# Feed-forward hidden tiles in parts of 4, 6, 6 and 6 in place of 4, 5, 6 and 7

## The chip, the cores and the metric

The kernel runs on one core of a Trainium2 chip. The metric is the device time of one execution, in microseconds (us). Three runs of the kernel before gave a median of 2325.38 us, from 2324.81 to 2325.91.

The engines are named as the profile names them: PE (TensorE, matmuls), PEld (its weight loads), ACT (ScalarE), DVE (VectorE), POOL (GpSimd) and SP (SyncE, which here issues nearly all transfers). Each engine works through its own list of instructions in order. They wait for each other through counting semaphores.

## What is computed

Four layers; each is a token mixer (attention, gated unit, pooling, attention) and a feed-forward part, all on 512 tokens of width 1024 in float32. Only the feed-forward part, whose hidden width is 2816, or 22 tiles of 128, is touched by the change:

```python
FFN_HIDDEN = -(-8 * D_MODEL // (3 * 256)) * 256          # 2816

def swiglu(h, w_gate_up, w_down):
    g, u = jnp.split(h @ w_gate_up, 2, axis=-1)
    return (jax.nn.silu(g) * u) @ w_down

# in reference(), once for each layer i
x = x + m
x = x + swiglu(rmsnorm(x, ffn_norm[i]), ffn_w_gate_up[i], ffn_w_down[i])
```

## The kernel before

**Precision.** Each float32 operand of a matmul is split into a high part, rounded by an ACT copy, and a low part, which DVE gets as the difference. A product is three matmuls: high by high, high by low, low by high. So every weight that a transfer brings passes ACT and then DVE before PE may use it.

**Parts.** The 22 hidden tiles of a layer are done in four parts, p = 0 to 3. A part first computes its hidden tiles (gate and linear columns, silu, product) and then multiplies them by its rows of `w_down`: eight blocks, one for each tile of the output, each added to `x` by DVE (`add`, line 1208). A block of a part of n tiles is 3n matmuls of 512 columns.

**Part 0** (4 tiles) computes gate and linear in the plain way, from the operand in `xs_hi`/`xs_lo`. Meanwhile ACT and DVE build from `x` the sums of token halves that the later parts need.

**Parts 1 to 3** compute each hidden tile as a *pair* (its gate and its linear columns) with seven products in place of eight (Winograd's form of Strassen's scheme). They are called s1, s2, a11, s4, s3, a12, a22, in this order. Each is 12 matmuls of 256 columns, so a pair is 84 matmuls. The weights of a pair are 512 rows of sums (`s32`, built by DVE in `pair_sums`, lines 1233 to 1239) and of raw columns. They are split in four *chunks* c = 0 to 3: the high part by ACT (`pair_high`, line 737), the low part by DVE (`pair_low`, line 1245). s1 and s3 read chunk 0, s2 and s4 chunk 1, a11 and a12 chunk 2, a22 chunk 3. ACT also copies four finished products out of PSUM (`snap`, line 814). PE waits for the first copy before s4, for the second before s3, for the third before a12 and for the fourth before a22.

**Two homes for a pair's split weights.** One is the ring of four slots `w_hi`/`w_lo`, which also holds the split weights of the `w_down` blocks. The other is the space of `xs_hi`/`xs_lo`, free after part 0's gate and linear blocks. The pairs of a part take turns, and the last must be in `xs`, since the ring is then needed for `w_down`:

```python
def pair_slot(p, j):                  # 1: xs_hi/xs_lo, 0: the ring
    return (PAIRS[p] - j) % 2
```

Chunk c of a part's first pair (j = 0) may be written at these points (in `pair_high`, lines 730 to 736; `plain_before(l, p)` counts the blocks up to the part's start, `block_done` those that PE has done):

```python
elif pair_slot(p, j) == 0:
    act.wait_ge(block_done, plain_before(l, p) - 3 + c)
elif c == 0:
    if p == 1:
        act.wait_ge(block_done, plain_before(l, 0))
    else:
        act.wait_ge(product_done, 7 * pair_at(l, p))
```

So in the ring, chunk c waits for the fifth, sixth, seventh and eighth `w_down` block of the part before, since each of these blocks reads one slot.

**The order around part 0's end** is written out by hand, in `first_tiles` of ACT and of DVE. `up` is the layer's first feed-forward block; the `w_down` blocks of part 0 are `up + 8` to `up + 15`. ACT, from line 794:

```python
split(up + 14, ...); pair_high(l, 1, 0, 0); pair_high(l, 1, 0, 1)
split(up + 15, ...); pair_high(l, 1, 0, 2); pair_high(l, 1, 0, 3)
```

DVE, from the sums of the first pair on:

```python
pair_sums(l, 1, 0); add(2); split(up + 14, ...); pair_low(l, 1, 0, 0)
add(3); split(up + 15, ...); token_part_low(2, 1); add(4)
pair_low(l, 1, 0, 1); pair_low(l, 1, 0, 2); add(5); pair_low(l, 1, 0, 3)
b21_low(); add(6); pair_sums(l, 1, 1); add(7)
```

After that ACT enters the loop over the part's pairs. For pair j it first splits chunk 0 of pair j + 1, then takes the first copy `snap(q, 2)`, splits chunks 1 and 2, takes the second copy `snap(q, 1)`, splits chunk 3, and takes the third and fourth copy. Chunk 0 and chunk 1 of pair j + 1 wait for `pair_sums` of that pair on DVE.

**Transfers.** SP loads raw pairs alternately into `raw_b` (even j) and `raw_a` (odd j). `raw_a` is the space of the two buffers `raw` for plain blocks, so the load of pair 1 of a part waits until DVE has split the last `w_down` block (`w_lo_ready`).

Of the kernel before, what the change touches and what calls it, by code (L numbers as in the profile page):

```python
# [37 lines left out]
HEADS, GROUPS, DH = 16, 4, 64  # L38
NCMP = 32
HIDDEN_TILES = 22  # L40
PARTS = (4, 5, 6, 7)
TILES_AT = (0, 4, 9, 15)
LAST_PART = len(PARTS) - 1
FIRST_TILES = PARTS[0]
PAIRS = (0, 5, 6, 7)
PAIRS_AT = (0, 0, 5, 11)
LAYER_PAIRS = sum(PAIRS)
H = 256
BW = 1024
# [9 lines left out]
MIX_BLOCKS = {"nsa": 38, "sgu": 25, "pool": 18}  # L59
FFN_BLOCKS = 2 * FIRST_TILES + MT * len(PARTS)  # L60

# [38 lines left out]
class Plan:  # L100
# [35 lines left out]
    def width(self, b):  # L136
# [3 lines left out]
        for at in self.ffn:  # L140
            p, k = divmod(b - at - 2 * FIRST_TILES, MT)
            if 0 <= p <= LAST_PART:
                return PARTS[p] * P
        return BW
# [13 lines left out]
def pair_at(l, p, j=0):  # L158

    return LAYER_PAIRS * l + PAIRS_AT[p] + j  # L160


def pair_slot(p, j):

    return (PAIRS[p] - j) % 2


def loads_before(q):

    l, r = divmod(q, LAYER_PAIRS)  # L170
    buf = [j % 2 for n in PAIRS for j in range(n)]
    return l * buf.count(buf[r]) + buf[:r].count(buf[r])
# [79 lines left out]
def build(nc, x_in, positions, stream, pairs, params, consts, b_s, out, mixers=MIXERS):  # L252
    plan = Plan(mixers)
    ctx = ExitStack()
    with ctx:  # L255
# [260 lines left out]
        def _(sp):  # L516
# [20 lines left out]
            def loads(lo, hi):  # L537
                for b in range(lo, hi):
                    if b in plan.plain:
                        load_plain(b)  # L540
                    else:
                        load(b, (b - plan.skipped(b)) % RAW)
# [15 lines left out]
            for l in range(len(mixers)):  # L558
# [3 lines left out]
                loads(up + 4, up + 2 * FIRST_TILES + MT)  # L562
                for p in range(1, len(PARTS)):
                    n = PAIRS[p]
                    for j in range(1, n):
# [99 lines left out]
        def _(act):  # L665
# [78 lines left out]
            def down_high(l, p, k):  # L744

                if k < RING:
                    act.wait_ge(product_done, 7 * (pair_at(l, p, PAIRS[p] - 2) + 1))
                b = plan.down_block(l, p) + k
# [52 lines left out]
            def ffn(l):  # L801
                n = norm_of_ffn(l)
                first_tiles(l)
                for p in range(1, len(PARTS)):
                    tiles = count = PARTS[p]
                    t0 = HIDDEN_TILES * l + TILES_AT[p] + tiles - count
                    down = plan.down_block(l, p)
# [311 lines left out]
        def _(dve):  # L1119
# [260 lines left out]
            def ffn(l):  # L1380
# [3 lines left out]
                for p in range(1, len(PARTS)):  # L1384
                    tiles = count = PARTS[p]
                    t0 = HIDDEN_TILES * l + TILES_AT[p] + tiles - count
                    down = plan.down_block(l, p)
# [511 lines left out]
        def _(pe):  # L1899
# [152 lines left out]
            def ffn(l):  # L2052
# [10 lines left out]
                for p in range(1, len(PARTS)):  # L2063
                    for j in range(PAIRS[p]):
                        pair(l, p, j)
                    down, t0 = plan.down_block(l, p), HIDDEN_TILES * l + TILES_AT[p]
                    for k in range(MT):
# [371 lines left out]
def _tiles(w, nk=MT):  # L2439

    K, M = w.shape
    b = w.reshape(K // P, P, M // P, P).transpose(2, 1, 0, 3).reshape(M // P, P, (K // P) * P)
    return _pad(b)
# [11 lines left out]
def _stream(i, mixers, total):  # L2455
    out = []
    for l, (kind, j) in enumerate(mixers):
# [26 lines left out]
        out.append(both.reshape(2 * FIRST_TILES, P, BW))  # L2484
        for n, t in zip(PARTS, TILES_AT):
            out.append(_tiles(down[t * P:(t + n) * P]))
# [85 lines left out]
```

## Time and profile before

| | |
|---|---|
| median of three runs | 2325.38 us |
| the profiled execution | 2326.84 us |
| its span, first to last instruction | 2325.0 us |
| PE busy | 2313.3 us, 99% |
| PEld busy | 2078.9 us, 89% |
| DVE busy | 1737.7 us, 75% |
| ACT busy | 1131.9 us, 49% |
| mean granted clock of TensorE | 0.999 |

The matmuls are pipelined and overlap in the records, so a short wait of PE need not show as idle time. It shows as a larger step from the start of one matmul to the start of the next: in steady work 0.227 us for 512 columns and 0.120 us for 256.

### The profile page before, as it was taken

The page shows a single profiled execution, that of the slowest core. Times are in us where ns is not written, and L with a number is a line of the kernel's source. Part 1 is how long each engine was busy: PE and PEld are TensorE (multiplying, and loading weights), DVE is VectorE, ACT ScalarE, POOL GpSimd, SP SyncE. Part 2 cuts the span into 40 slices and gives each one's busy share as a digit, 9 for nine tenths or more (in the row PEclk, how much of TensorE's full clock was granted, in tenths as well). Part 3 has the DMA queues.
Part 4 walks back from the last instruction along what each step waited for, and adds up shares of the span by engine and source line. Part 5 has one row for each costly group of instructions (what it writes and reads, how often), then busy time and mean ns, then how long its engine had stood idle before and what let it go on. Part 6 is the DMA issues. An engine that isn't in the chain of part 4 may idle for free.

```text
span 2325.0 us, 37973 instructions
## 1 busy us (share of the span) xinstructions
PE 2313.3 (99%) x14360; PEld 2078.9 (89%) x14360; DVE 1737.7 (75%) x2847; ACT 1131.9 (49%) x1944; POOL 308.1 (13%) x305
## 2 busy tenths in 40 slices
PE   9999999999999999999999999999999999999998
PEld 7889988999988889999988899998889998899997
DVE  8667668876965679687777897696756776978693
ACT  6268744544543335454533454454326783454453
POOL 2211140000030120000123000003320114000003
PEclk9999999999999999999999999999999999999999
DMA  4820013333323233333233333332470003223332
GB/s 160 220 64 2 1 56 100 114 96 102 114 84 102 89 108 100 99 109 110 78 97 100 99 111 100 95 116 84 123 209 28 1 2 98 89 93 102 98 101 84
DMA packets 69295, 217.38 MB, mean 93 GB/s; under 512 B 8193, under 2 KB 8321, under 8 KB 69121
## 3 DMA queue, kind: packets, MB, share of 16 engines
q1 hardware_dynamic: 62928, 204.39, 27.7%
q0 software_dynamic: 5184, 8.40, 1.8%
q8 instruction: 116, 1.90, 0.3%
q10 hardware_dynamic: 1008, 2.21, 0.3%
q14 instruction: 59, 0.48, 0.1%
HBM read 204.48 MB, written 2.10 MB: 89 GB/s over the span
## 4 chain that ended last, share of the span: by engine, by line
PE 77%; DVE 0%; ACT 0%; issue 0%; DVEq 0%; ACTq 0%
PE bank L1901 76%; PE bank L2241 2%; PE bank L2271 0%; DVE branch L1666 0%; DVE big L1894 0%; ACT L695 0%; DVE w_lo L1245 0%; ACT w_hi L737 0%; ACT xg L1108 0%; DVE act_t L1398 0%; DVE x L1208 0%; DVEq L255 0%; DVE rden L1661 0%; DVE rden L1663 0%; PE bank L2145 0%
## 5 line engine op out<-in xcount | busy, mean ns | idle before, releaser
L679 ACT ACTIVATE w_hi<-raw 128x1024 fp32r<-128x1024 f32 (+4 forms) x260 | 239.6, 922 | 297.0 <-DMA raw<-stream 238.3
L1141 DVE TENSOR_TENSOR w_lo<-raw,w_hi 128x1024 fp32r<-128x1024 f32 (+4 forms) x257 | 287.9, 1126 | 112.8 <-ACT w_hi L679 112.4
L1901 PE MATMUL bank<-hid_hi,w_hi 128*128 128x512 f32 x720 | 280.9, 390 | 0.0
L1901 PE MATMUL bank<-hid_lo,w_hi 128*128 128x512 f32 x720 | 280.5, 390 | 0.0
L1901 PE MATMUL bank<-hid_hi,w_lo 128*128 128x512 f32 x720 | 280.3, 389 | 0.0
L1901 PE MATMUL bank<-xs_hi,w_hi 128*128 128x512 f32 (+2 forms) x720 | 279.2, 388 | 0.8 <-DVE w_lo L1141 0.5
L1901 PE MATMUL bank<-xs_lo,w_hi 128*128 128x512 f32 (+2 forms) x720 | 273.4, 380 | 0.0
L1901 PE MATMUL bank<-xs_hi,w_lo 128*128 128x512 f32 (+1 forms) x704 | 267.5, 380 | 0.0
L1208 DVE TENSOR_TENSOR x<-bank,x 128x512 f32<-128x512 f32 (+1 forms) x160 | 110.2, 689 | 198.7 <-PE bank L1901 198.3
L1901 PE MATMUL bank<-mix_hi,w_hi 128*128 128x256 f32 (+1 forms) x768 | 246.0, 320 | 0.0
L1901 PE MATMUL bank<-mix_hi,w_lo 128*128 128x256 f32 (+1 forms) x768 | 244.8, 319 | 0.0
L1901 PE MATMUL bank<-mix_lo,w_hi 128*128 128x256 f32 (+1 forms) x768 | 244.8, 319 | 0.0
L595 POOL TENSOR_TENSOR work<-x 128x512 f32<-128x512 f32 x8 | 15.0, 1877 | 1390.6 <-DVE x L1208 1306.7
L814 ACT ACTIVATE part_sums<-bank 128x256 f32<-128x256 f32 x288 | 108.5, 377 | 165.7 <-PE bank L1901 165.4
L1642 DVE CUSTOM_DVE_ANT_0 attn<-bank,causal_b 128x512 f32<-128x512 f32 (+3 forms) x256 | 118.8, 488 | 84.7 <-PE bank L1901 83.9
L1901 PE MATMUL bank<-mix_hi,xs_hi 128*128 128x256 f32 x640 | 181.3, 283 | 0.2 <-DVE w_lo L1245 0.2
L1901 PE MATMUL bank<-mix_hi,xs_lo 128*128 128x256 f32 x640 | 181.3, 283 | 0.0
L1901 PE MATMUL bank<-mix_lo,xs_hi 128*128 128x256 f32 x640 | 181.3, 283 | 0.0
L1901 PE MATMUL bank<-tmp,attn 128*128 128x65 f32 x1280 | 162.8, 268 | 0.0
L1901 PEld LDWEIGHTS bank<-xs_hi,w_hi 128*128 128x128 f32 (+1 forms) x720 | 135.1, 188 | 29.4 <-DVE xs_lo L1149 1.5
L1901 PEld LDWEIGHTS bank<-hid_hi,w_hi 128*128 128x128 f32 x720 | 135.2, 188 | 29.2 <-DVE hid_lo L1405 1.5
L1901 PEld LDWEIGHTS bank<-hid_hi,w_lo 128*128 128x128 f32 x720 | 135.2, 188 | 28.0
(280 smaller groups left out, 5878.8 us busy)
## 6 DMA issues: line engine op xcount, KB each, us to landing
raw<-stream SPq DMA_DIRECT2D x131, 512.0 KB, 3.7
raw_b<-pairs SPq DMA_DIRECT2D x80, 512.0 KB, 4.8
raw_a<-pairs SPq DMA_DIRECT2D x64, 512.0 KB, 4.6
raw<-stream SPq DMA_DIRECT2D x32, 448.0 KB, 3.4
raw<-stream SPq DMA_DIRECT2D x32, 384.0 KB, 3.1
raw<-stream SPq DMA_DIRECT2D x32, 320.0 KB, 2.9
w_f<-stream SPq DMA_DIRECT2D x18, 512.0 KB, 3.7
raw<-stream SPq DMA_DIRECT2D x34, 256.0 KB, 2.6
```

Of the source, the lines that this page charges most:

```text
L595: gp.tensor_tensor(work[:, 0, :], x[:, 0, :], x[:, 0, :], ALU.mult).then_inc(sq_step, 1)
L679: nc.scalar.activation(w_hi[:, slot, 0:n], raw[:, k, 0:n], ACT.Copy).then_inc(w_hi_ready, 1)
L814: nc.scalar.activation(part_sums[:, i, :], src[:, 0:H], ACT.Copy).then_inc(snapped, 1)
L1141: nc.vector.tensor_tensor(w_lo[:, slot, 0:n], raw[:, k, 0:n], f32(w_hi[:, slot, 0:n]), ALU.subtract).then_inc(w_lo_ready, counted(b))
L1208: nc.vector.tensor_tensor(tile(x, m), bank[slot][:, :], tile(x, m), ALU.add).then_inc(taken, 1)
L1642: nc.vector.tensor_tensor_reduce(out=prob[:, p % 4, bass.ts(j, w)], in0=bank[score_bank(l0, p)][:, bass.ts(j, w)], in1=causal_b[:, S - w:S ...
L1901: return nc.tensor.matmul(out_, w, v, start=start, stop=stop, skip_group_check=onto)
L2241: last = nc.tensor.transpose(bank[turn_bank(l0, p)][:, bass.ts(k, P)], prob[:, p % 4, bass.ts(k, P)], ident[:, :])
```

## The change

```diff
-PARTS = (4, 5, 6, 7)
-TILES_AT = (0, 4, 9, 15)
+PARTS = (4, 6, 6, 6)
+TILES_AT = (0, 4, 10, 16)
 LAST_PART = len(PARTS) - 1
 FIRST_TILES = PARTS[0]
-PAIRS = (0, 5, 6, 7)
-PAIRS_AT = (0, 0, 5, 11)
+PAIRS = (0, 6, 6, 6)
+PAIRS_AT = (0, 0, 6, 12)
```

The number of pairs of a layer (18), of blocks and of matmuls stays. A tile moves from the last part to the first of the three; the widths of `w_down`'s blocks follow (640, 768 and 896 columns become 768 each). Since 5 and 7 are odd and 6 is even, `pair_slot(p, 0)` goes from 1 to 0 in parts 1 and 3: their first pair moves from `xs` to the ring, and with it every later pair of part 1 and of part 3 changes home.

ACT, at the end of part 0 in layer 0, before (line 679 splits a plain block, 737 a chunk of a pair, 814 is the copy of a product out of PSUM; `block_done` counts PE's blocks):

```order
L679 ACTIVATE w_hi<-raw 128x512 [waits block_done,raw_full1]
L737 ACTIVATE xs_hi<-s32_58 128x1024 [waits block_done,s_ready]
L737 ACTIVATE xs_hi<-s32_58 128x1024 [waits s_ready]
L679 ACTIVATE w_hi<-raw 128x512 [waits block_done,raw_full0]
L737 ACTIVATE xs_hi<-raw_b 128x1024 [waits pair_full_b]
L737 ACTIVATE xs_hi<-raw_b 128x512
L737 ACTIVATE w_hi<-s32_58 128x1024 [waits block_done,s_ready]
L814 ACTIVATE part_sums_63<-bank45 128x256 [waits product_done,hid_full]
```

The same place on ACT now:

```order
L679 ACTIVATE w_hi<-raw 128x512 [waits block_done,raw_full1]
L737 ACTIVATE w_hi<-s32_58 128x1024 [waits block_done,s_ready] x2
L679 ACTIVATE w_hi<-raw 128x512 [waits block_done,raw_full0]
L737 ACTIVATE w_hi<-raw_b 128x1024 [waits block_done,pair_full_b]
L737 ACTIVATE w_hi<-raw_b 128x512 [waits block_done]
L737 ACTIVATE xs_hi<-s32_58 128x1024 [waits block_done,s_ready]
L814 ACTIVATE part_sums_63<-bank45 128x256 [waits product_done,hid_full]
```

No instruction changes its place; the four chunks of the first pair go to `w_hi`, and each of them now waits for a block of PE, where before only the first did, and for a much earlier one.

DVE, a little behind it in the program, as the difference of the two (line 1293 is `token_part_low`, 1208 `add`, 1245 `pair_low`, 1312 `b21_low`):

```order
 L1293 TENSOR_TENSOR b_lo_60<-b32_59,b22_hi_61 128x1024
 L1208 TENSOR_TENSOR x<-bank2,x 128x512
-L1245 TENSOR_TENSOR xs_lo<-s32_58,xs_hi 128x1024
-L1245 TENSOR_TENSOR xs_lo<-raw_b,xs_hi 128x1024
-L1208 TENSOR_TENSOR x<-bank3,x 128x512
-L1245 TENSOR_TENSOR xs_lo<-raw_b,xs_hi 128x512
+L1245 TENSOR_TENSOR w_lo<-s32_58,w_hi 128x1024
+L1245 TENSOR_TENSOR w_lo<-raw_b,w_hi 128x1024
+L1208 TENSOR_TENSOR x<-bank3,x 128x512
+L1245 TENSOR_TENSOR w_lo<-raw_b,w_hi 128x512
 L1312 TENSOR_TENSOR b_lo_60<-b32_59,xs_hi 128x512
 L1312 TENSOR_TENSOR b_lo_60<-b32_59,xs_lo 128x512
```

Here too the order stands as it was; the low parts go to `w_lo`, and each follows ACT's high part of the same chunk.

## Rows read from the trace of the kernel before

**Rows 1.** The page, part 1: busy us, share of the span, instructions
```profile
PE 2313.3 (99%) x14360; PEld 2078.9 (89%) x14360; DVE 1737.7 (75%) x2847; ACT 1131.9 (49%) x1944; POOL 308.1 (13%) x305
```

**Rows 2.** Waits of PE, longest first: total us, times, longest
```profile
PE bank L2145 <- ACT tmp L890: 1.6, 1, 1.6
```

**Rows 3.** Windows of layer 0: busy of PE, PEld, DVE, ACT, POOL; clock; DMA
```profile
395.14:416.90 21.76, 21.76 (x97) 18.03 (x96) 21.49 (x29) 8.09 (x12) 0.00 (x0) 1.00 0.36 111
416.90:467.30 50.40, 50.40 (x422) 50.39 (x421) 42.54 (x59) 28.32 (x53) 0.00 (x0) 1.00 0.32 105
467.30:494.78 27.48, 27.48 (x123) 22.45 (x121) 16.98 (x22) 7.41 (x9) 0.00 (x0) 1.00 0.27 86
```

**Rows 4.** Timeline of PE, layer 0: start us, us, instruction
```profile
395.14 0.39 PE L1901 MATMUL bank<-hid_hi,w_hi 128*128 128x512 f32 x1
...
416.90 0.28 PE L1901 MATMUL bank<-mix_hi,xs_hi 128*128 128x256 f32 x1
...
421.22 0.28 PE L1901 MATMUL bank<-b_hi,xs_hi 128*128 128x256 f32 x1
```

**Rows 5.** Timeline of DVE, layer 0, part 0's end and part 1's first pair
```profile
406.95 1.22 DVE L1245 TENSOR_TENSOR xs_lo<-s,xs_hi 128x1024 fp32r<-128x1024 f32 x1
...
408.68 0.68 DVE L1141 TENSOR_TENSOR w_lo<-raw,w_hi 128x512 fp32r<-128x512 f32 x1
...
416.29 1.22 DVE L1233 TENSOR_TENSOR s<-raw_a 128x1024 f32<-128x1024 f32 x1
...
427.92 0.69 DVE L1398 TENSOR_TENSOR act_t<-act_t,lin 128x512 f32<-128x512 f32 x1
```

**Rows 6.** Timeline of ACT, the same stretch; in brackets idle before, and releaser
```profile
407.01 0.62 ACT L679 ACTIVATE w_hi<-raw 128x512 fp32r<-128x512 f32 x1
...
417.54 1.06 ACT L737 ACTIVATE w_hi<-s 128x1024 fp32r<-128x1024 f32 x1 [8.44 <-DVE s L1233]
418.60 0.38 ACT L814 ACTIVATE part_sums<-bank 128x256 f32<-128x256 f32 x1
418.99 1.06 ACT L737 ACTIVATE w_hi<-s 128x1024 fp32r<-128x1024 f32 x1
419.96 1.05 ACT L737 ACTIVATE w_hi<-raw_a 128x1024 fp32r<-128x1024 f32 x1
420.91 0.36 ACT L814 ACTIVATE part_sums<-bank 128x256 f32<-128x256 f32 x1
...
421.69 0.37 ACT L814 ACTIVATE part_sums<-bank 128x256 f32<-128x256 f32 x1
...
431.34 0.38 ACT L814 ACTIVATE part_sums<-bank 128x256 f32<-128x256 f32 x1
```

**Rows 7.** Timeline of ACT, layer 0, part 1's end: part 2's first pair
```profile
491.64 1.06 ACT L737 ACTIVATE w_hi<-raw_b 128x1024 fp32r<-128x1024 f32 x1 [1.68 <-PE bank L1901]
494.98 0.64 ACT L737 ACTIVATE w_hi<-raw_b 128x512 fp32r<-128x512 f32 x1 [2.28 <-PE bank L1901]
```

**Rows 8.** Timeline of PE, layer 0: part 1's first `w_down` block; part 2's second pair
```profile
469.82 0.39 PE L1901 MATMUL bank<-hid_hi,w_lo 128*128 128x512 f32 x1
...
470.50 0.39 PE L1901 MATMUL bank<-hid_lo,w_hi 128*128 128x512 f32 x1
...
510.49 0.28 PE L1901 MATMUL bank<-b_hi,xs_lo 128*128 128x256 f32 x1
...
511.14 0.28 PE L1901 MATMUL bank<-mix_lo,xs_hi 128*128 128x256 f32 x1
```

**Rows 9.** The transfers into `raw_a`, by tile; and DVE's timeline at part 2
```profile
DMA to landing us min/median/max: 3.8/4.6/6.5
503.62 1.23 DVE L1233 TENSOR_TENSOR s<-raw_b 128x1024 f32<-128x1024 f32 x1 [0.81 <-DMA raw_b<-pairs]
```

**Rows 10.** PE's longest wait, layer 0's mixer: timeline, and its window
```profile
114.87 0.44 PE L2145 MATMUL bank<-ident,tmp 128*128 128x128 f32 x2 [1.55 <-ACT tmp L890]
112.00:120.00 8.00, 6.45 (x34) 4.44 (x33) 5.04 (x7) 2.90 (x5) 0.00 (x0) 1.00 0.43 137
```

## The prediction

> **What bounds the kernel now.** I read the page first, then PE's waits, then the windows of one layer's parts, then the timelines of PE, DVE and ACT side by side at the borders between parts. PE is busy for 99% of the span [rows 1], and its longest wait in the whole trace is 1.6 us [rows 2]. Busy time alone would prove little, because the matmuls overlap in the records, so I look at steps from start to start. Five pairs of part 1 take 50.40 us [rows 3], which is 10.08 us a pair, 84 steps of 0.120, 1.44 us a product. The eight `w_down` blocks of part 0 run from 395.14 to 416.90 [rows 4], 2.72 us each, 12 steps of 0.227. There is nothing between them. PE sets the time here, and the change leaves its matmuls as they are. So it can cost or give only what PE waits at borders.
>
> The second thing to see is how near DVE is to its limit at the border that the change touches. In the window of part 0's `w_down` blocks DVE is busy for 21.49 of 21.76 us [rows 3]. From 408.68 (the low split of the eighth block) to 416.29 (`pair_sums` of part 1's second pair) it works without a gap [rows 5]. ACT has 8.09 us to do in the same window, and PE still never waits. In the pairs behind it DVE has 42.54 of 50.40 us [rows 3].
>
> **What goes.** Two small waits of PE end with the part of 5 tiles. In its first `w_down` block the fifth tile's input is late: two steps take 470.50 − 469.82 = 0.68 us in place of 2 × 0.227 [rows 8], so 0.23 us are lost. It stands at the same two matmuls of this part in each of the four layers. With 6 tiles the input is asked for three matmuls, 0.68 us, later. That gives 4 × 0.23 = 0.92 us. In layer 0, part 2's second pair also loses 511.14 − 510.49 − 2 × 0.12 = 0.41 us [rows 8]. It hangs on a late transfer (in part 2, DVE waits 0.81 us for `raw_b` [rows 9]), whose issue waits on the first pair's last chunk on DVE. Behind blocks of 6 tiles, DVE has 0.68 us more per block before that point, so I count these 0.41 us as gone too. Together 1.33 us. The last part's blocks become shorter by 3 matmuls, the first part's longer by as many; PE's sum over them is the same, so they stand at nothing.
>
> **What comes: part 1's first pair must wait for the ring.** I work it out in layer 0; the other layers hold the same instructions. Part 0's fifth to eighth blocks end at 408.74, 411.46, 414.18 and 416.90 (416.90 less 3, 2, 1 and 0 blocks of 2.72). A chunk's high copy starts 0.20 to 0.29 us behind its block where a first pair already lies in the ring: in part 2, 494.98 behind the last block's end at 494.78, and 491.64 behind the seventh's at 494.78 − 27.48 / 8 = 491.35 [rows 3, 7]. I take 0.25.
>
> - DVE comes to the low part of chunk 0 at 406.95 as before [rows 5], but ACT's copy can start only at 408.99 and takes 1.06. So DVE stands still from 406.95 to 410.05.
> - ACT is in order: chunk 1 is queued ahead of the eighth block's split. Chunk 1 starts at 411.46 + 0.25 = 411.71. The split follows 0.97 later (418.99 to 419.96 is such a step) at 412.68, and takes 0.62 [rows 6]: 413.30. DVE, which has `add(3)` behind it by 411.8, stands still again until 413.33.
> - From this split to `pair_sums` of the second pair DVE has the same ten instructions as before, 416.29 − 408.68 = 7.61 us [rows 5]. Chunks 2 and 3 do not hold it up: their copies are done by 415.5 and 417.8, and DVE, with the lengths of rows 5 (1.22 for 1024 columns, 0.68 for 512, of which some 0.08 overlap), comes to them at about 416.8 and 418.5. `pair_sums` starts at 413.33 + 7.61 = 420.94, which is 4.65 us later than before.
> - ACT waits for it, and with ACT the copies out of PSUM. Chunk 0 of the second pair started 1.25 us behind `pair_sums` (417.54), the first copy 1.06 later (418.60, 0.38 long) [rows 6]. With 4.65 us more the first copy ends at 423.63. PE wants to begin the fourth product, s4, at 421.22 [rows 4]. It waits 2.43 us with 0.02 for the signal.
> - The second copy, at 420.91 + 4.65, ends at 425.92 [rows 6]. PE is through s4 at 423.65 + 1.44 = 425.09 and wants s3: another 0.85 us. The third copy (421.69) ends at 426.71, before s3 is done at 427.38, so a12 does not wait. The first pair ends at 416.90 + 10.08 + 3.28 = 430.26.
> - In the second pair PE is 3.28 late and DVE 4.65, since from `pair_sums` to the product of silu and linear (416.29 to 427.92 [rows 5]) it had no gap to make good. The second copy of this pair, 431.34 to 431.72 before [rows 6], ends at 436.37. PE wants s3 at 430.26 + 4 × 1.44 = 436.02: 0.37 us. From there on DVE's spare time (7.86 us in five pairs) takes up the rest.
>
> In sum 2.43 + 0.85 + 0.37 = 3.65 us a layer, 14.6 in four layers. The eighth block's low split is now done at 414.02 where PE wants it at 414.18. That leaves 0.16 us of cover, so I put it at nothing, with up to 0.1 us a layer beyond. What cover is there elsewhere: chunks 0 to 2 are ready at least 1.4 us before their products ask for them, and chunk 3 earlier still.
>
> **Parts 2 and 3.** Part 2's first pair was in the ring already. Part 3's moves there. But at this border the order by hand has chunks 0 and 1 behind the sixth block's `add`, chunk 2 behind the seventh's, chunk 3 behind the eighth's. So the ring's wait is one that DVE mostly passes in any case, and in part 2 PE loses nothing for it in the first pair. I take zero, with 0 to 0.4 us a layer (the loss in rows 8) as bounds.
>
> **The sum.** 14.6 − 1.33 = 13.3 us. The profiled execution took 2326.84, 1.84 beyond its span of 2325.0; the median of the runs is 1.46 lower. The terms are differences within one execution, so I add them to the median: 2325.4 + 13.3 = 2338.7 us, 0.57% more.
>
> **Rivals.**
>
> *The wait is hidden, as at part 2.* Place: ACT's first copy in part 1's first pair. It costs PE nothing if that copy ends by 421.22, so if `pair_sums` starts by 421.22 − 0.38 − 1.06 − 1.25 = 418.53. My 420.94 would have to be 2.4 us too late. For it: in part 2 the same slots are waited for, and PE goes on. Against it: in part 2 `pair_sums` stands ahead of chunk 3, and here it stands behind all four chunks, two splits of other data and an `add`. Price: only the gains are left, 2325.4 − 1.3 = 2324.1 us, not slower. Chance 0.06.
>
> *The transfer of the second pair becomes the bound.* Its place `raw_a` is free when the eighth block is split, which moves from before 409.4 to 414.02. Such a load takes 3.8 to 6.5 us, 4.6 in the median [rows 9], so it lands between 417.8 and 420.5, and DVE asks for it at 420.94. For it: DVE did wait for a pair's transfer at part 2 [rows 9]. Against it: even the longest of 64 is in time. If it took 1 us more than the time that it has, 7.9 us, the loss would be 1 us a layer: 2342.7. Chance 0.10.
>
> *PE loses its fast clock in the wait.* Behind its longest wait before, 1.55 us, the granted clock of the window stayed at 1.00 [rows 10], its upper level of 2.4 GHz, and a wait of 2.43 us is not in the trace. The Trainium skill ("TensorE: Matmul & The Clock Gate", Part 1) holds that throttled is the default state of the array and that only activity keeps it fast. By that rule the time would be higher; the one row here that bears on it shows no loss. If the 2.4 GHz fell to 1.2 for one pair, that would be 10.08 us a layer: 2338.7 + 40 = 2379 us. Chance 0.03.
>
> *Less of it:* the second and third wait fail to come because ACT gets by sooner than I count; then 4 × 2.43 − 1.33 = 8.4, 2333.8 us. Chance 0.10, inside or just below the range.
>
> **How the numbers follow.** My forecast has 0.71; with the three other slower cases (0.10, 0.03, 0.10) slower has 0.94. No difference beyond 0.2%, 4.7 us, is about what a measurement here can tell from none. The hidden wait, 0.06, falls within it, but for 0.01 that I leave for faster: nothing in the rows gives 4.7 us back. The range goes from 2334.0 (the first wait alone) to 2343.0 (the late transfer); it leaves out the hidden wait and the clock.
>
> **What would show it.** On DVE two gaps before the low parts of chunk 0 and of the eighth block, about 3.1 and 1.5 us, and no gap then until `pair_sums` on `raw_a`, some 4.0 us behind part 1's start in place of 0.6 before it. On PE a step of about 2.5 us before the fourth product of part 1's first pair, one of about 1 before the fifth, and a small one before the fifth of the second pair, in all four layers. PE's waits name ACT's copies (line 814) with eight or more entries. The fifth tile's two steps are gone. I am wrong if the first pair of part 1 stays at 10.1 us, if part 2 or 3 shows waits of that size, or if the clock in these windows is under 1.

## The result, and the profile after

The changed kernel takes 2340.14 us in the median (2339.66 to 2340.93), against 2325.28 for the kernel before in the same session: a ratio of 1.0064, 95% interval 1.0047 to 1.0081. It is 14.9 us slower; 13.3 were forecast, and 2340.14 lies in the range. The profiled execution took 2339.66 us, its span is 2337.8.

The page looks almost as before. Its first part, in the same columns:

```profile
PE 2316.3 (99%) x14360; PEld 2081.0 (89%) x14360; DVE 1740.5 (74%) x2847; ACT 1134.6 (49%) x1944; POOL 305.0 (13%) x305
```

Set beside [rows 1], the engines have as many instructions as before, and PE is busy for 3.0 us more where the span grew by 12.8. What grew is the time between. Windows of layer 0, in the columns of [rows 3]: part 0's `w_down` blocks, the first and the second pair of part 1, its other four pairs, its `w_down` blocks:

```profile
393.28:415.08 21.80, 21.80 (x98) 17.94 (x96) 17.11 (x23) 7.91 (x11) 0.00 (x0) 1.00 0.23 68
415.08:428.56 13.48, 10.53 (x86) 10.18 (x85) 13.37 (x17) 6.11 (x11) 0.00 (x0) 1.00 0.43 139
428.56:439.04 10.48, 10.31 (x87) 10.13 (x86) 10.13 (x14) 6.00 (x11) 0.00 (x0) 1.00 0.38 125
439.04:479.36 40.32, 40.32 (x339) 40.32 (x338) 33.44 (x48) 23.06 (x43) 0.00 (x0) 1.00 0.32 108
479.36:512.02 32.66, 32.66 (x146) 27.04 (x145) 18.38 (x23) 7.95 (x9) 0.00 (x0) 1.00 0.27 81
```

The first pair takes 13.48 us in place of 10.08, the second 10.48, the other four 10.08 each. DVE's busy time in part 0's blocks fell from 21.49 [rows 3] to 17.11: work that it no longer gets done there lies in the first pair, where it is now busy for 13.37 of 13.48 us. The timeline of DVE shows where it stood still. In brackets: idle before, and what ended it.

```profile
404.55 0.68 DVE L1141 TENSOR_TENSOR w_lo<-raw,w_hi 128x512 fp32r<-128x512 f32 x1
408.24 1.23 DVE L1245 TENSOR_TENSOR w_lo<-s,w_hi 128x1024 fp32r<-128x1024 f32 x1 [3.00 <-ACT w_hi L737]
409.38 0.68 DVE L1208 TENSOR_TENSOR x<-bank,x 128x512 f32<-128x512 f32 x1
411.48 0.69 DVE L1141 TENSOR_TENSOR w_lo<-raw,w_hi 128x512 fp32r<-128x512 f32 x1 [1.41 <-ACT w_hi L679]
...
419.10 1.21 DVE L1233 TENSOR_TENSOR s<-raw_a 128x1024 f32<-128x1024 f32 x1
```

The two gaps are there, 3.00 and 1.41 us. `pair_sums` on `raw_a` starts 4.02 us behind part 1's start at 415.08; before, it started 0.61 us ahead of it [rows 4, 5]. There is no idle time in front of it, so the transfer into `raw_a` was in place. ACT, over the same border:

```profile
407.14 1.06 ACT L737 ACTIVATE w_hi<-s 128x1024 fp32r<-128x1024 f32 x1 [3.61 <-PE bank L1901]
409.86 1.06 ACT L737 ACTIVATE w_hi<-s 128x1024 fp32r<-128x1024 f32 x1 [1.66 <-PE bank L1901]
...
420.34 1.06 ACT L737 ACTIVATE xs_hi<-s 128x1024 fp32r<-128x1024 f32 x1 [4.43 <-DVE s L1233]
421.30 0.37 ACT L814 ACTIVATE part_sums<-bank 128x256 f32<-128x256 f32 x1
...
423.70 0.36 ACT L814 ACTIVATE part_sums<-bank 128x256 f32<-128x256 f32 x1
```

Chunks 0 and 1 wait for PE's blocks. Before, with part 1's start at 416.90, ACT had both done by 407.1, in one go and with no wait in front:

```profile
405.12 1.99 ACT L737 ACTIVATE xs_hi<-s 128x1024 fp32r<-128x1024 f32 x2
```

In the changed kernel ACT then waits 4.43 us for `pair_sums` of the second pair, and the two copies out of PSUM (line 814) stand behind it. PE goes on 0.10 and 0.11 us after they end:

```profile
419.27 0.28 PE L1901 MATMUL bank<-b_hi,w_lo 128*128 128x256 f32 x1
421.77 0.36 PE L1901 MATMUL bank<-b_hi,w_hi 128*128 128x256 f32 x1 [2.22 <-issue]
421.96 0.28 PE L1901 MATMUL bank<-b_lo,w_hi 128*128 128x256 f32 x1
...
423.16 0.28 PE L1901 MATMUL bank<-b_hi,w_lo 128*128 128x256 f32 x1
424.17 0.36 PE L1901 MATMUL bank<-mix_hi,w_hi 128*128 128x256 f32 x1 [0.73 <-DVE xs_lo L1245]
```

A step of 2.50 us in place of 0.12, and one of 1.01; each has a step of 0.19 behind it. PE's waits as the view lists them (total us, times, longest):

```profile
PE bank L1901 <- issue: 9.2, 5, 2.2
PE bank L1901 <- DVE xs_lo L1245: 1.5, 2, 0.7
```

The view does not name ACT's copies. It has "issue" for the long waits and a DVE instruction for the second one, because several semaphores are waited for there. The ACT and PE timelines side by side point to the copies, and e4 below bears it out: with the copies taken early, these two waits are gone.

Two layers hold something more. The windows of part 1's first pair in layer 2 and in layer 3:

```profile
1353.46:1367.42 13.96, 11.74 (x85) 11.56 (x84) 13.82 (x18) 6.11 (x11) 0.00 (x0) 0.88 0.45 141
2041.78:2056.16 14.38, 11.82 (x85) 11.38 (x84) 14.21 (x19) 6.11 (x11) 0.00 (x0) 0.88 0.48 151
```

The granted clock (the column before the DMA share) is 0.88 there, and 0.50 for a stretch of it, in layer 2 this one:

```profile
1360.00:1363.40 3.40, 3.25 (x15) 3.28 (x16) 3.40 (x5) 3.12 (x6) 0.00 (x0) 0.50 0.04 16
```

Four matmuls of layer 2's first pair in PE's timeline:

```profile
1360.15 0.55 PE L1901 MATMUL bank<-b_hi,w_hi 128*128 128x256 f32 x1 [2.22 <-issue]
1360.50 0.41 PE L1901 MATMUL bank<-b_lo,w_hi 128*128 128x256 f32 x1
1360.71 0.41 PE L1901 MATMUL bank<-b_hi,w_lo 128*128 128x256 f32 x1
...
1363.47 0.28 PE L1901 MATMUL bank<-mix_hi,w_hi 128*128 128x256 f32 x1
```

Behind the wait the steps are 0.213 us in place of 0.120, as long as the clock stands at 0.50, or 1.2 GHz in place of 2.4; from 1363.47 on they are 0.120 again.

### The profile page after: what moved, and what is told of

Read it like the earlier page. It is cut to its first block, busy times and chain, and to the rows that moved or that the text cites. A ratio compares the mean times of both kernels' runs of the same rounds, so it can differ in the third digit from the quotient of the medians.

```text
span 2337.8 us, 37973 instructions
## 1 busy us (share of the span) xinstructions
PE 2316.3 (99%) x14360; PEld 2081.0 (89%) x14360; DVE 1740.5 (74%) x2847; ACT 1134.6 (49%) x1944; POOL 305.0 (13%) x305
## 4 chain that ended last, share of the span: by engine, by line
PE 60%; DVE 0%; issue 0%; ACT 0%; DVEq 0%; ACTq 0%
PE bank L1901 58%; PE bank L2241 2%; PE bank L2271 0%; DVE branch L1666 0%; DVE big L1894 0%; ACT L695 0%; DVE w_lo L1245 0%; ACT w_hi L737 0%; ACT xg L1108 0%; DVE x L1208 0%; DVE act_t L1398 0%; DVE rden L1661 0%; DVEq L255 0%; DVE rden L1663 0%; PE bank L2145 0%
## 5 line engine op out<-in xcount | busy, mean ns | idle before, releaser
L679 ACT ACTIVATE w_hi<-raw 128x1024 fp32r<-128x1024 f32 (+2 forms) x260 | 239.8, 923 | 306.5 <-DMA raw<-stream 237.5
L1141 DVE TENSOR_TENSOR w_lo<-raw,w_hi 128x1024 fp32r<-128x1024 f32 (+2 forms) x257 | 290.1, 1134 | 118.1 <-ACT w_hi L679 117.5
L1901 PE MATMUL bank<-mix_hi,w_hi 128*128 128x256 f32 (+1 forms) x832 | 264.7, 318 | 1.8 <-DVE xs_lo L1245 1.5
L1901 PE MATMUL bank<-mix_lo,w_hi 128*128 128x256 f32 (+1 forms) x832 | 263.2, 316 | 0.0
L1901 PE MATMUL bank<-mix_hi,w_lo 128*128 128x256 f32 (+1 forms) x832 | 263.2, 316 | 0.0
L1901 PEld LDWEIGHTS bank<-mix_hi,w_hi 128*128 128x128 f32 x832 | 159.3, 191 | 12.9 <-DVE xs_lo L1245 2.4
L1901 PEld LDWEIGHTS bank<-mix_hi,w_lo 128*128 128x128 f32 x832 | 159.1, 191 | 10.2
L1901 PEld LDWEIGHTS bank<-mix_lo,w_hi 128*128 128x128 f32 x832 | 159.2, 191 | 10.0
L1901 PE MATMUL bank<-mix_hi,xs_lo 128*128 128x256 f32 x576 | 163.0, 283 | 0.0
L1901 PE MATMUL bank<-mix_lo,xs_hi 128*128 128x256 f32 x576 | 163.0, 283 | 0.0
```

Source lines behind the costliest of these rows:

```text
L679: nc.scalar.activation(w_hi[:, slot, 0:n], raw[:, k, 0:n], ACT.Copy).then_inc(w_hi_ready, 1)
L1141: nc.vector.tensor_tensor(w_lo[:, slot, 0:n], raw[:, k, 0:n], f32(w_hi[:, slot, 0:n]), ALU.subtract).then_inc(w_lo_ready, counted(b))
L1901: return nc.tensor.matmul(out_, w, v, start=start, stop=stop, skip_group_check=onto)
```

## The experiments

All times are medians, with the ratio to the kernel before on the same chip and its 95% interval.

**One border at a time.** The theory: all of the loss comes from part 1's first pair. The rival: a first pair in the ring costs at each border. Two other splittings of the tiles have one of the two borders each:

```diff
-PARTS = (4, 6, 6, 6)
+PARTS = (4, 6, 5, 7)      # e1: part 1's first pair in the ring, part 3's in xs
+PARTS = (4, 5, 7, 6)      # e2: part 3's first pair in the ring, part 1's in xs
```

> Parts of 4, 6, 5, 7: of the two borders that the change moves to the ring, only part 1's first pair is there; part 3's stays in xs. My theory (the loss is all at part 1's first two pairs): 3.8 us a layer as in the changed kernel, four times, 15.3; the late fifth tile is back, now in part 2 (no gain of 0.92), layer 0's 0.41 is gone: 2325.3 + 14.9 = 2340.2 us, up to 0.6 more if the clock falls again in two layers. Rival, that each of the two first pairs in the ring costs its share: 2325.3 + 7.4 = 2332.7 us.

Measured: 2343.96 us, 1.0082 (1.0068 to 1.0096). Layer 1, the first pair of part 1 and of part 3:

```profile
905.84:919.32 13.48, 10.52 (x85) 10.16 (x84) 13.38 (x17) 6.11 (x11) 0.00 (x0) 1.00 0.45 145
1080.67:1090.74 10.07, 10.07 (x85) 10.07 (x84) 9.68 (x13) 5.34 (x10) 0.00 (x0) 1.00 0.57 178
```

The whole loss is at part 1. The time is 3.2 us above the upper end of my expectation. In the profiled execution (2341.93 us) the clock fell in three layers, not two. The five runs follow the mean granted clock: 2341.65 us at 0.999, 2341.93 and 2343.96 at 0.997, 2345.24 at 0.995, 2346.60 at 0.994. What the slower of them look like inside was not recorded.

> Parts of 4, 5, 7, 6: only part 3's first pair is in the ring, part 1's and part 2's are in xs. My theory: no wait at part 3's border, 10.08 us a pair everywhere, the late fifth tile of part 1 as before: 2325 us, between 2324.4 and 2326. Rival, that a first pair in the ring costs wherever it stands: 2332.7 us.

Measured: 2324.69 us, 0.9997 (0.9988 to 1.0006). ACT's timeline before part 3 in layer 1:

```profile
1082.88 1.06 ACT L737 ACTIVATE w_hi<-raw_b 128x1024 fp32r<-128x1024 f32 x1 [3.70 <-PE bank L1901]
1087.58 0.63 ACT L737 ACTIVATE w_hi<-raw_b 128x512 fp32r<-128x512 f32 x1 [3.64 <-PE bank L1901]
```

and the windows of part 3's first two pairs:

```profile
1087.38:1097.45 10.07, 10.07 (x85) 10.06 (x84) 9.68 (x13) 5.90 (x11) 0.00 (x0) 1.00 0.61 189
1097.45:1107.53 10.08, 10.08 (x86) 10.08 (x85) 9.65 (x13) 6.00 (x11) 0.00 (x0) 1.00 0.33 104
```

ACT waits 3.70 and 3.64 us for the ring, and PE loses nothing here; over the four layers, only layer 2's second pair of part 3 is longer, by 0.11 us. So being in the ring is not by itself what costs. Two things differ at this border: DVE is busy for only 19.77 of the 38.11 us of part 2's blocks, and `pair_sums` stands ahead of chunk 3, so that it starts 2.26 us ahead of part 3's start at 1087.38:

```profile
1085.12 1.22 DVE L1233 TENSOR_TENSOR s<-raw_a 128x1024 f32<-128x1024 f32 x1
```

e6 below brings the second to part 1's border, without the first.

**The eighth block's split ahead of chunk 0.** If the transfer into `raw_a`, or the split of the eighth block, is what comes late, this takes the loss away; if it is DVE's order, only the second gap's share.

```diff
 # ACT                                    # DVE
+split(up + 15, ...)                      +add(3); split(up + 15, ...)
 pair_high(l, 1, 0, 0)                     pair_low(l, 1, 0, 0)
 pair_high(l, 1, 0, 1)                    -add(3); split(up + 15, ...)
-split(up + 15, ...)                       token_part_low(2, 1)
```

> The changed kernel, but the eighth w_down block of part 0 is split ahead of chunk 0 of the first pair, on ACT and on DVE. The load into raw_a goes out some 6 us sooner; DVE still stands before chunk 0, but not a second time. My theory (DVE comes late to pair_sums, PE pays for it through ACT's copies): pair_sums starts 0.85 us sooner, the first wait of PE falls from 2.45 to about 1.6 us, the other two (0.96 and 0.41) stay: 4 x 0.85 = 3.4 us less than the changed kernel, 2336.7 us. Rival, that the load into raw_a is what is late: all of the waits go, 2325 us. Rival, that the split of the eighth block on PE's side is what is late: 2325 us too.

Measured: 2336.28 us, 1.0046 (1.0033 to 1.0060). DVE and PE in layer 1:

```profile
897.73 1.23 DVE L1245 TENSOR_TENSOR w_lo<-s,w_hi 128x1024 fp32r<-128x1024 f32 x1 [1.85 <-ACT w_hi L737]
...
907.82 1.21 DVE L1233 TENSOR_TENSOR s<-raw_a 128x1024 f32<-128x1024 f32 x1
910.49 0.36 PE L1901 MATMUL bank<-b_hi,w_hi 128*128 128x256 f32 x1 [1.49 <-issue]
```

The load into `raw_a` now goes out 8.62 us ahead of part 1's start, in place of 2.89. `pair_sums` starts 907.82 − 904.53 = 3.29 us behind that start, 0.73 sooner than in the changed kernel (4.02), and PE's first wait shrinks by as much (2.22 to 1.49). DVE was now idle in front of chunks 2 and 3 too, for 1.34 and 0.41 us. Both rivals, which had all of the waits go, fall. The first pair is 12.75 us in all four layers, at a clock of 1.00; in layer 1:

```profile
904.53:917.28 12.75, 10.53 (x85) 10.18 (x84) 12.24 (x16) 6.11 (x11) 0.00 (x0) 1.00 0.33 101
```

**ACT's copies ahead of the next pair's chunks.** PE waits for copies that stand behind a late chunk on ACT. Is ACT's order the cause, or only the place where PE meets DVE's lateness?

```diff
+if p == 1 and j == 0:
+    snap(q, 2, ...); snap(q, 1, ...); snap(q, 0, ...)
 pair_high(l, p, j + 1, 0)
-snap(q, 2, ...)              # for this pair; likewise snap(q, 1) and snap(q, 0) below
```

> The changed kernel, but in part 1's first pair ACT takes the first three copies out of PSUM ahead of the next pair's chunks, so the copies no longer stand behind pair_sums. Rival (ACT's order is the cause: the copies are only queued behind a chunk that is late): the waits before the fourth and fifth product go, 3.4 us a layer, 2340.1 - 13.6 = 2326.5 us. My theory (DVE is late by 4.65 us against before, and the copies are only the first place where PE meets that): the waits move to the last product of the first pair, to the start of the second pair and into it, and the sum stays: about 3.8 us a layer, 2340 us, 2338 at the least.

Measured: 2339.33 us, 1.0062 (1.0048 to 1.0076). All waits of PE in the first two pairs of layer 1 (the same lines stand 9 lower in this kernel: 1910 is 1901):

```profile
914.00 0.36 PE L1910 MATMUL bank<-mix_hi,w_hi 128*128 128x256 f32 x1 [0.88 <-DVE xs_lo L1254]
916.82 0.36 PE L1910 MATMUL bank<-mix_hi,xs_hi 128*128 128x256 f32 x1 [1.17 <-DVE lin L1442]
921.74 0.35 PE L1910 MATMUL bank<-b_hi,xs_hi 128*128 128x256 f32 x1 [0.38 <-ACT part_sums L814]
923.91 0.35 PE L1910 MATMUL bank<-mix_hi,xs_hi 128*128 128x256 f32 x1 [0.50 <-DVE w_lo L1254]
```

The waits before the fourth and fifth product are gone. Four others have come, at the last product of the first pair, at the start of the second and inside it. Together the two pairs take 12.50 + 11.47 = 23.97 us, as in the changed kernel (13.47 + 10.49 in its layer 1). It is DVE's lateness that PE pays, by whatever way it reaches PE.

**DVE given work while it waits, and `pair_sums` at two places.** Both kernels have the eighth block's split as in e3, and `token_part_low` and `b21_low` ahead of chunk 0. They differ in the place of `pair_sums`, and two `add` stand one chunk later in e6:

```diff
 # DVE in e5                               # DVE in e6
 add(3); split(up + 15, ...)               add(3); split(up + 15, ...)
+token_part_low(2, 1); b21_low()          +token_part_low(2, 1); b21_low()
 pair_low(l, 1, 0, 0); add(4)              pair_low(l, 1, 0, 0); add(4)
 pair_low(l, 1, 0, 1); add(5)              pair_low(l, 1, 0, 1)
 pair_low(l, 1, 0, 2); add(6)             +pair_sums(l, 1, 1)
 pair_low(l, 1, 0, 3)                      pair_low(l, 1, 0, 2); add(5)
 pair_sums(l, 1, 1)                        pair_low(l, 1, 0, 3); add(6)
 add(7)                                    add(7)
```

> The changed kernel with ACT's and DVE's hand-written order at part 0's end moved: the eighth block's split, token_part_low and b21_low ahead of chunk 0, so that DVE has work while it waits for the ring; pair_sums of the second pair still behind chunk 3. My theory: DVE's two gaps cost nothing now, but chunk 3 waits for the last w_down block, so pair_sums starts about 1.5 us behind part 1's start in place of 4.0; the first wait of PE goes, about 0.7 us stay before the fifth product and 0.4 in the second pair: 2325.3 - 1.3 + 4 x 1.1 = 2328.4 us. Rival (any first pair in the ring costs PE a wait for its weights, whatever DVE's order): near 2340 us.

Measured: 2329.48 us, 1.0013 (1.0004 to 1.0022). Chunk 3 and `pair_sums` in DVE's timeline of layer 1:

```profile
903.38 0.69 DVE L1245 TENSOR_TENSOR w_lo<-raw_b,w_hi 128x512 fp32r<-128x512 f32 x1 [0.41 <-ACT w_hi L737]
904.00 1.22 DVE L1233 TENSOR_TENSOR s<-raw_a 128x1024 f32<-128x1024 f32 x1
```

and the window of the first pair:

```profile
902.52:913.46 10.94, 10.30 (x85) 10.12 (x84) 10.43 (x13) 6.11 (x11) 0.00 (x0) 1.00 0.39 116
```

`pair_sums` starts 1.48 us behind part 1's start. The first wait is gone and 0.86 us stay in the first pair, 0.41 in the second: chunk 3's wait for the last block, by itself.

> As the kernel with the moved order, but pair_sums of the second pair stands right behind chunk 1, ahead of chunks 2 and 3. My theory: pair_sums starts some 2.8 us ahead of part 1's start (0.6 ahead in the kernel before), no wait of PE at any border, 10.08 us for each of the 72 pairs, and the late fifth tile and layer 0's 0.41 us are gone: 2325.3 - 1.3 = 2324.0 us, 1.3 us under the kernel before, which may not be told from it. Clock at 1.00 in all four layers. Rival (the ring itself costs): above 2328 us.

Measured: 2325.62 us, 0.9997 (0.9988 to 1.0006), where the kernel before took 2326.11. `pair_sums` in DVE's timeline of layer 1:

```profile
898.89 1.23 DVE L1233 TENSOR_TENSOR s<-raw_a 128x1024 f32<-128x1024 f32 x1
```

and the windows of the first and the second pair:

```profile
901.64:911.71 10.07, 10.07 (x85) 10.06 (x84) 9.97 (x13) 5.90 (x11) 0.00 (x0) 1.00 0.48 136
911.71:921.91 10.20, 10.20 (x86) 10.13 (x85) 9.88 (x14) 6.00 (x11) 0.00 (x0) 1.00 0.34 117
```

With the same tiles and the same ring, but `pair_sums` 2.75 us ahead of part 1's start, the loss is all but gone. 0.12 us stay in the second pair (0.33 in layer 3), which I had not expected. The kernel is as fast as the one before; the 0.5 us between them cannot be told from nothing.

**A longer wait, for the clock.** In e7 `pair_sums` stands behind `add(7)`; in e8 the first copy also stands behind the next pair's chunk 1 on ACT:

```diff
-add(6); pair_sums(l, 1, 1); add(7)        # DVE, e7 and e8
+add(6); add(7); pair_sums(l, 1, 1)
-snap(q, 2, ...); pair_high(l, p, j + 1, 1)     # ACT, e8, first pair of part 1
+pair_high(l, p, j + 1, 1); snap(q, 2, ...)
```

> The changed kernel with pair_sums of the second pair one instruction later on DVE, behind add(7). By waits alone: the first wait of PE grows from 2.45 to about 3.1 us, the second stays at 0.96, the third goes; 4.1 us a layer, 2325.3 - 1.3 + 16.5 = 2340.5 us. If PE's clock depends on the length of one wait: half clock in all four layers (two of four in the changed kernel's trace, with 2.45 us; none where the wait was 1.66), and up to 1 us a layer on top: 2341 to 2345 us, with a wide spread from run to run.

Measured: 2343.88 us, 1.0080 (1.0062 to 1.0098). In layer 0 the first two pairs take 4.1 us more than two pairs without a wait, as by waits alone, and the clock stays at 1.00. In the other three layers it falls, and they take 4.8 to 5.1 us more. I had expected it to fall in all four.

> As the kernel with pair_sums behind add(7), and the first copy out of PSUM of part 1's first pair stands behind the next pair's chunk 1 on ACT. By waits alone: one wait of about 4.6 us a layer and no second one, 4.6 to 4.7 us a layer: 2325.3 - 1.3 + 18.6 = 2342.6 us. If the clock depends on the length of one wait: half clock behind it in all four layers, for at least 3.4 us each as in the changed kernel's records, so 1 to 2 us a layer on top: 2346 to 2351 us.

Measured: 2350.33 us, 1.0106 (1.0088 to 1.0124). The first pair in layers 0 and 2:

```profile
415.58:432.68 17.10, 12.65 (x85) 12.46 (x84) 15.36 (x20) 6.11 (x11) 0.00 (x0) 0.80 0.47 162
1360.09:1376.14 16.05, 11.59 (x86) 11.41 (x85) 15.37 (x20) 6.11 (x11) 0.00 (x0) 0.89 0.51 165
```

The clock falls in all four layers, and the loss is 6.0 to 7.0 us in each. The wait is 4.6 us of it, a step of 4.73 us in place of 0.12; the rest comes with the half clock.

## Why the prediction was right, point by point

- **PE bounds the kernel and only waits at borders count.** Held. The feed-forward parts of the four layers took 1206.2 us before and 1220.9 in the changed kernel, from the first `w_down` block to the last: 14.7 us of the 14.9. The two profiled executions differ by some 1.9 us less than that because the changed one reached layer 0's feed-forward part 1.9 us sooner, at 393.28 in place of 395.14 [rows 4]. The instructions up to there are the same in both; most of it is PE's wait of [rows 10], which the changed kernel's profile does not have.
- **Part 1's first pair.** Held, step for step: the gaps on DVE (3.1 and 1.5 forecast, 3.00 and 1.41 measured), `pair_sums` 4.04 us behind the part's start (4.02), the waits before the fourth and fifth product and the small one in the second pair, in layers 0 and 1 (for layers 2 and 3 see the clock, below). e1 shows that the whole of it is at this border, e5 and e6 that it goes with the place of `pair_sums`, e4 that ACT's order only decides where PE meets it. Set side by side, for a start of `pair_sums` 4.02, 3.29 and 1.48 us behind the part's start and 2.75 us ahead of it, the first two pairs lost 3.8, 3.1, 1.3 and 0.1 us (changed kernel, e3, e5, e6).
- **The size of that term** was a little low: 2.43 + 0.85 + 0.37 = 3.65 us a layer, and 2.45 + 0.96 + 0.41 = 3.82 in layers 0 and 1. The difference is mostly the slower step behind each wait, 0.07 us, which I had left out, three times. The sum's 0.02 us for the signal has no row behind it: from the end of a copy to PE's next start it was 0.10 and 0.11. That the first wait still came out right has some luck in it, since the first copy ended 6.59 us behind the part's start, where the sum had 6.73. The net loss is 14.9 us in place of 13.3: about 0.7 us by these sizes, 0.6 by the clock, 0.25 in part 3 of layer 2 and 0.1 in part 0's blocks.
- **The eighth block's split** had 0.16 us of cover by my count. Part 0's blocks took 21.80 us, 0.04 more than before, inside the bound of 0.1; in e3, with this split earlier, they took 21.76 again.
- **What goes** went. The parts of 6 tiles run their blocks in 32.67 us without the two long steps of [rows 8], and layer 0's 0.41 us are gone. In their place layer 2 lost 0.25 us in part 3's second pair, inside the bound of 0 to 0.4 that I gave parts 2 and 3. DVE waited 1.34 us for the transfer into `raw_b` there, as in [rows 9].
- **The rivals.** The hidden wait is out: 2.4 us too little cover, as worked out. The late transfer is out: DVE has no gap before `pair_sums`, in the changed kernel and in e3, where the load went out 5.7 us sooner. *PE loses its fast clock* had a chance of 0.03 at a price of one pair a layer, and the truth lies between. This part of the prediction failed: a wait of 1.55 us that had cost nothing [rows 10] said nothing of one of 2.4. The clock did fall in two layers of the profiled execution, but the slow matmuls cost about 0.09 us each and there were only some 16 in each. And much of it was not paid twice: while PE is slow, DVE catches up, and the wait in the second pair is gone. Layer 2 lost 0.08 us more than layer 1 by it, layer 3 lost 0.51. That the time stayed in the range in spite of it is in part luck: e1 has the same waits at this border and only 0.9 us more to pay for its fifth tile, and three of its five runs were above the range's upper end of 2343.0.
- **What the profile would show** held on DVE, and on PE in layers 0 and 1. Three points failed. PE's waits do not name ACT's copies. The smaller steps did not come in all four layers: layer 2 has neither, layer 3 has 0.76 us before the fifth product and none in the second pair. And I had named a clock under 1 in these windows as a sign that I am wrong: it was 0.88 in layers 2 and 3. The wait and its path stand without it, but not the assumption that PE pays for the wait alone.

## What to carry to other kernels

When a buffer's home changes, the new wait need not be where the loss appears. Follow the in-order engine that now stands still: what is queued behind its wait, who waits for that, and how much slack each had in the trace before. The same wait was free where the engine had idle time and the step that others need did not stand behind all of it (part 3), and dear where the engine was full and that step came last (part 1). Before giving up such a change, move work that does not depend on the wait ahead of it, and the step that others need out from behind it: with both, e6 was as fast as the kernel before.

## What was not expected of the hardware

One wait of PE can cost it its fast clock. At a step of about 2.50 us the granted clock fell to 0.50, in or behind the wait, in two of four layers of the changed kernel and in three of four of e1; at 3.2 us (e7) in three of four; at 4.7 us (e8) in four of four. In e3 the longest step is 1.76 us: the clock stays at 1.00 in all four layers. It does so in e4 too, where the waits of the two pairs add up to the same 3.8 us as in the changed kernel and the longest step is 1.45 us. So in these runs the clock fell only at a single long wait. e4 also spreads its waits over a longer stretch than the changed kernel does, and whether short waits close together would do the same is not shown. Which layers were hit at 2.50 us differs between the changed kernel (2 and 3) and e1 (0, 2 and 3), whose waits are alike; what decides it is not shown. The Trainium skill ("TensorE: Matmul & The Clock Gate", Part 1) has it that the array is throttled by default and only activity keeps it fast; the clock of 0.50 behind these waits agrees with that.
